# Hybrid mixer block on one core: the linear mixer's loop on 64x64 tiles, the state-space mixer's masked sums made once, and the delta rule's closing part inside the next mixer's projection

## The chip, the cores and the metric

The program runs on one core of one Trainium2 chip. The metric is the device time of one execution in microseconds, lower being better. TensorE is called PE here, its weight loads PEld, VectorE DVE, ScalarE ACT, GpSimd POOL and SyncE SP. All data is float32.

## The reference, cut to what matters

One transformer-like block: four token mixers of 256 channels each read the same normed activations (256 context tokens and 1024 tokens, 10 tiles of 128), and a mixture of experts with 64 experts follows. The change touches the mixers only. Each is a recurrence run forward and backward over chunks of 64 tokens, with 4 heads of 64 channels.

```python
def gla_core(q, k, v, gk, s0):                       # the linear mixer
    b = jnp.cumsum(gk, axis=3)
    q_t, k_t, k_s = q * jnp.exp(b), k * jnp.exp(-b), k * jnp.exp(b_last - b)
    att = jnp.where(incl, jnp.einsum('bnhid,bnhjd->bnhij', q_t, k_t), 0.0)
    o_intra = jnp.einsum('bnhij,bnhjv->bnhiv', att, v)
    def step(s, xs):
        o_n = jnp.einsum('bhid,bhdv->bhiv', q_n, s)
        s = s * dec_n[..., None] + jnp.einsum('bhjd,bhjv->bhdv', k_n, v_n)

def ssd_core(x, a, bm, cm, s0):                      # the state-space mixer
    acum = jnp.cumsum(ac, axis=-1)
    seg = acum[..., :, None] - acum[..., None, :]
    lmat = jnp.exp(jnp.where(incl, seg, -jnp.inf))
    dte = jnp.exp(acum[..., -1:] - acum)
    cd = jnp.exp(acum[..., -1])

def deltanet_mixer(...):                             # the gated delta rule
    o, st = bidir(gdn_core, ...)
    y = head_rms(o, lp['dn_norm_g']) * jax.nn.silu(z)
```

## The kernel before, in words

The mixers run one after the other as phases: `gla` (linear mixer), `mamba` (state-space mixer), `deltanet` (gated delta rule), `rwkv`. A phase ends with a barrier of all engines and the freeing of its semaphores; inside it there are blocks, and every block also starts and ends together on all engines. Each engine runs its own list of instructions, written out by hand in program order, and waits on counting semaphores. All buffers lie in one `arena`; PSUM is eight banks of 128x512, `k.ps[0]` to `k.ps[7]`. A float32 product shows in the trace as two loads and two matmuls, so 16 products of the program are 32 rows there.

A mixer first projects the activations (long rows of 128x512 products) and then runs a loop over 10 steps `i`. In each step two tiles of 128 tokens are handled, one forward (`d = 0`) and one backward (`d = 1`). Steps 0 and 1 are context and only move the state; steps 2 to 9 are `live` and also give outputs.

**Linear mixer loop (L527 to L724).** PE does, per live step: `cumulate(i + 2)` (L499), `scores(i, 0)` (L544), `updates(i)` (L558), `scores(i, 1)`, and for each direction `turn(i + 1, d)` (L536) and `results(i, d)` (L569 and L575). A pair of 64-token chunks is treated as one 128x128 tile: the scores of a head are a 128x128 product of which the mask `k.glamask` keeps the two diagonal blocks; to hold the two heads of a pair apart, the turned queries `QT` are stored with zeros in the other head's rows, by three ACT copies a direction (L635 to L637). DVE masks the scores (L686), moves the state through both chunks (L697 to L713), scales the next queries and keys (`scale`, L656 and L658) and copies the results out (L722). ACT also makes the exponents (L602, L603). PE's `scores` of direction 0 comes before `updates`, and the mask of direction 0 stands before the state work on DVE.

**State-space loop (L1016 to L1146).** Per step and direction, `sums(i, d)` makes three narrow products of the decays with masks (L1022: inclusive, strict and all-ones), then, if live, four 128x128 products (L1026) and two grams (L1031). DVE copies the narrow sums to `SM` (L1102) and caps four differences (`capped`, L1106). ACT takes the exponential `EX` of the sums (L1081), makes `XD` (L1076, inputs times step size) and `XE` (L1085, `XD` times a column of `EX`), and the exponential of the capped differences (L1090). DVE multiplies (`mix`, L1112) and, after PE's `products(i, d)` (L1047, L1050, L1055), closes the step (`close`, L1120 to L1129). PE's order is sums(i+1,0), products(i,0), sums(i+1,1), products(i,1); `sums(i+1,d)` waits for `mix(i,d)`, because both use the banks `k.ps[d]` and `k.ps[2+d]`.

**Delta rule's closing part (`turned_out`, L2038 to L2090).** After the loop's block a block of its own squares, sums and norms the output (DVE, L2079 to L2083), turns it with 64 products (PE, L2071), gates it (DVE, L2089) and writes it to `mixed_turned` (SP, L2059). Then the phase ends and `rwkv` starts: SP loads the low-rank weights `WL` (L2141), and PE needs them for its first products (L2165, L2169). The projection `mains` is L2226, with the narrow `logits` (L2183, L2186) in between.

## Time and profile before

| | us |
|---|---|
| median of three executions | 2696.27 (2692.99 to 2698.2) |
| the profiled execution, its time | 2702.41 |
| its span in the trace | 2700.5 |
| PE busy in the span | 2483.4 |
| DVE busy | 1513.2 |
| ACT busy | 983.5 |
| POOL busy | 830.1 |

The profiled execution has its own time, 1.9 us above its span and 6.1 us above the median. Time stamps in rows count from the start of the span. "Busy" of PE includes matmuls that stream one behind the other, and so says that PE has work, not that it works at its peak. Granted clock 1.00 is 2.4 GHz and 0.50 is 1.2 GHz.

### The profile page before, as it was taken

The page shows a single profiled execution, that of the slowest core. Times are in us where ns is not written, and L with a number is a line of the kernel's source. Part 1 is how long each engine was busy: PE and PEld are TensorE (multiplying, and loading weights), DVE is VectorE, ACT ScalarE, POOL GpSimd, SP SyncE. Part 2 cuts the span into 40 slices and gives each one's busy share as a digit, 9 for nine tenths or more (in the row PEclk, how much of TensorE's full clock was granted, in tenths as well). Part 3 has the DMA queues.
Part 4 walks back from the last instruction along what each step waited for, and adds up shares of the span by engine and source line. Part 5 has one row for each costly group of instructions (what it writes and reads, how often), then busy time and mean ns, then how long its engine had stood idle before and what let it go on. Part 6 is the DMA issues. An engine that isn't in the chain of part 4 may idle for free. (4 is left out here: it accounts for less than half of the span.)

```text
span 2700.5 us, 72223 instructions
## 1 busy us (share of the span) xinstructions
PE 2483.4 (92%) x27163; PEld 1367.8 (51%) x27164; DVE 1513.2 (56%) x2615; ACT 983.5 (36%) x1707; POOL 830.1 (31%) x656
## 2 busy tenths in 40 slices
PE   4999999999799699899879779899999999999976
PEld 2447548745599545799734343233333333333332
DVE  3105464854578603566534566566666666666538
ACT  3513214512222113333211125455555555555422
POOL 1000000000255100111000005566666666666564
PEclk9999998998999899899989889999999999999989
DMA  6001222020000110000123237999989899684177
GB/s 241 28 0 51 92 65 66 33 94 32 2 4 4 38 39 0 3 5 4 55 94 105 113 142 310 340 347 359 359 322 343 332 342 345 254 306 153 71 285 299
DMA packets 109434, 410.20 MB, mean 152 GB/s; under 512 B 20953, under 2 KB 37035, under 8 KB 84140
## 3 DMA queue, kind: packets, MB, share of 16 engines
q1 hardware_dynamic: 76972, 289.81, 29.3%
q0 software_dynamic: 20736, 75.51, 7.2%
q10 hardware_dynamic: 11520, 41.95, 3.9%
q8 instruction: 153, 2.51, 0.4%
q14 instruction: 53, 0.43, 0.0%
HBM read 347.45 MB, written 59.77 MB: 151 GB/s over the span
## 5 line engine op out<-in xcount | busy, mean ns | idle before, releaser
L3323 PE MATMUL bank<-arena 128*32 x1280 | 568.9, 598 | 10.5 <-SPq L68 7.6
L3325 PE MATMUL bank<-arena 128*32 128x512 f32 x3840 | 570.0, 598 | 0.0
L3284 POOL COPY arena<-arena 128x2048 f32 x240 | 448.7, 1903 | 332.1 <-PE bank L3357 326.7
L3323 PEld LDWEIGHTS bank<-arena 128*32 128x32 f32 x1280 | 134.9, 110 | 359.5 <-issue 350.4
L3354 PE MATMUL bank<-arena 128*32 x640 | 289.4, 595 | 5.5 <-POOL arena L3284 5.5
L3357 PE MATMUL bank<-arena 128*32 128x512 f32 x1920 | 290.4, 595 | 0.0
L3478 DVE COPY arena<-arena 128x2048 f32 x80 | 134.8, 1684 | 206.8 <-PE bank L3325 188.4
L3415 ACT COPY arena<-arena 128x2048 f32 x80 | 152.2, 1902 | 169.0 <-PE bank L3325 140.7
L3274 POOL DMA_INDIRECT arena<-normed_rows,arena x80 | 164.2, 2053 | 118.3 <-DVE arena L3462 106.3
L1281 PE MATMUL bank<-arena 64*64 64x64 f32 x4480 | 165.8, 220 | 13.8 <-DVE arena L1353 5.4
L3354 PEld LDWEIGHTS bank<-arena 128*32 128x32 f32 x640 | 70.3, 110 | 197.9 <-issue 197.4
L1281 PEld LDWEIGHTS bank<-arena 64*64 64x64 f32 x4480 | 151.2, 136 | 19.3 <-DVE arena L1353 6.5
L3421 ACT COPY arena<-arena 128x2048 f32 x80 | 152.2, 1903 | 0.0
L3325 PEld LDWEIGHTS bank<-arena 128*32 128x32 f32 x3840 | 150.7, 110 | 0.0
L1522 PE MATMUL bank<-arena 128*128 128x512 f32 (+1 forms) x320 | 132.3, 570 | 0.0
L3456 DVE TENSOR_SCALAR arena<-bank,arena 128x128 f32<-128x128 f32 x320 | 109.0, 402 | 40.1 <-PE bank L3308 40.1
L512 PE MATMUL bank<-arena 128*128 128x512 f32 (+1 forms) x320 | 127.3, 552 | 0.0
L2508 POOL TENSOR_TENSOR arena<-arena 128x512 f32<-128x512 f32 x10 | 12.8, 1283 | 368.9 <-DVE arena L2574 255.0
L3390 ACT ACTIVATE arena<-bank,arena 128x128 f32<-128x128 f32 x320 | 121.7, 468 | 3.4 <-PE bank L3308 3.4
L1400 DVE SCALAR_TENSOR_TENSOR arena<-arena 128x945 f32<-128x945 f32 (+2 forms) x96 | 113.8, 1220 | 1.7
L2793 PE MATMUL bank<-arena 128*128 128x512 f32 x256 | 112.2, 596 | 0.0
L1353 DVE TENSOR_TENSOR arena<-arena,bank 128x512 f32<-128x512 f32 x100 | 68.5, 685 | 68.9 <-PE bank L1281 68.3
(554 smaller groups left out, 4457.3 us busy)
## 6 DMA issues: line engine op xcount, KB each, us to landing
arena<-in_exp_w_gate_dram SPq DMA_DIRECT2D x64, 1024.0 KB, 6.3
arena<-in_exp_w_up_dram SPq DMA_DIRECT2D x64, 1024.0 KB, 9.0
arena<-in_exp_w_down_dram SPq DMA_DIRECT2D x64, 1024.0 KB, 9.8
expert_rows<-arena ACTq DMA_DIRECT2D x80, 512.0 KB
arena<-in_w_mod_dram SPq DMA_DIRECT2D x32, 512.0 KB, 4.5
arena<-in_x_dram SPq DMA_DIRECT2D x16, 512.0 KB, 5.7
arena<-in_w_mod_dram SPq DMA_DIRECT2D x8, 1024.0 KB, 18.4
arena<-in_w_in_dram SPq DMA_DIRECT2D x4, 1536.0 KB, 10.2
```

The source lines that it names most:

```text
L512: last = nc.tensor.matmul(k.ps[p % 4][:, 0:width], k.hT[:, c, t * P:(t + 1) * P], W[g][:, c, ws], start=(c == 0), stop=(c == KC - 1))
L1281: last = self.nc.tensor.matmul(self.banks[bank][r, x * HD:(x + 1) * HD], lhsT[r, x], rhs[r, x], start=True, stop=True)
L1522: last = nc.tensor.matmul(k.ps[p % 4][:, 0:w], W[m // 3 % 2][:, c, (m % 3) * P:(m % 3 + 1) * P], k.hT[:, c, a:a + w], start=(c == 0), stop ...
L3274: nc.gpsimd.indirect_dma_start(out=G[:, b.q], out_offset=None, in_=xn_dram, in_offset=bass.IndirectOffsetOnAxis(ap=ID[:, b.q], axis=0)).th ...
L3284: last = nc.gpsimd.tensor_copy(down_copy(u), down_of(slots[u]))
L3323: nc.tensor.matmul(out(SUB - 1), XTT[:, b.q, c, rows(SUB - 1)], W[:, :, c], start=first, stop=end)
L3325: last = nc.tensor.matmul(out(u), XTT[:, b.q, c, rows(u)], WC[:, u, :, c], start=first, stop=end)
L3354: nc.tensor.matmul(ps[6 + half][rows(SUB - 1), :], HT[:, b.q, f, rows(SUB - 1)], W[:, f, c], start=(f == 0), stop=(f == 1))
L3357: last = nc.tensor.matmul(ps[6 + half][rows(u), :], HT[:, b.q, f, rows(u)], WDC[:, u, f, c], start=(f == 0), stop=(f == 1))
L3415: nc.scalar.copy(copy_of(2, LOW), part_of(slot, LOW)).then_inc(lo_a, 1)
L3421: nc.scalar.copy(copy_of(2, HIGH), part_of(slot, HIGH)).then_inc(hi_a, 1)
L3478: nc.vector.tensor_copy(copy_of(0, LOW), part_of(slots[0], LOW))
```

## The change

Three independent edits, in four phases.

1. **Linear mixer.** Scores, results within the chunk and results from the state are made head by head and chunk by chunk, as 64x64 products. `QT` with its zeros and `KT` become one buffer `QKT`, filled by one ACT copy a direction. PE's order becomes updates, scores, cumulate, both turns, results. `results` is now one group for both directions in two halves: the inner one (into bank 4) waits for the masks, and ACT copies it to the output `O`; the part from the state (into the upper half of banks 2 and 3, `px`) waits for the middle state, and DVE adds it to `O`. The masks move behind the middle state on DVE. Because `px` shares its banks with the scores `pa`, `scores(i)` waits for the addition of the step before (`result_out`).
2. **State-space mixer.** All masked sums of all steps are made at the loop's start by five products (`mask_sums`), then one DVE copy, three ACT exponentials and one DVE product (`XS`, the scale of `XE`). `sums` has no narrow products left and is left out for steps 0 and 1; `XE` is made from `T` and `XS`, `XD` only in live steps, and `XE` not in the last step.
3. **Delta rule and rwkv.** The block `turned_out` is gone. Its work becomes the class `TurnedPost`, called inside rwkv's projection: the norm at the start of DVE's list, the turning behind the first four `mains` products on PE, in bank 7, the gating on DVE and the writing at the end of SP's list. `logits` therefore rotates over three banks instead of four. The low-rank weights `WL` are loaded by SP during the delta rule's loop. ACT waits for the written `mixed_turned` before the copy of the first product of `m == 4`, the thirteenth.

```diff
@@ linear mixer, PE @@
-            def scores(i, d):
-                pe.wait_ge(turned_out, 2 * (i - CT) + d + 1)
-                for h in range(NH):
-                    q = h // 2
-                    last = nc.tensor.matmul(pa[d][:, h * P:(h + 1) * P], KT[:, i % 2, d, q * P:(q + 1) * P],
-                                            QT[:, i % 2, d, h * P:(h + 1) * P], start=True, stop=True)
+            def scores(i):
+                pe.wait_ge(turned_out, 2 * (i - CT) + 2)
+                if i > CT:
+                    pe.wait_ge(result_out, i - CT)
+                for d in range(2):
+                    for q in range(2):
+                        for a in range(2):
+                            r = slice(HD * a, HD * a + HD)
+                            for c in range(2):
+                                j = slice(64 * c, 64 * c + 64)
+                                last = nc.tensor.matmul(pa[a][j, d, q], QKT[r, i % 2, d, (2 + q) * P + 64 * c:(2 + q) * P + 64 * c + 64],
+                                                        QKT[r, i % 2, d, q * P + 64 * c:q * P + 64 * c + 64],
+                                                        start=True, stop=True)
...
+            def results(i):
+                pe.wait_ge(masked, i - CT + 1)
+                if i > CT:
+                    pe.wait_ge(inner_out, i - CT)
...
+                            last = nc.tensor.matmul(po[j, d, h // 2, h % 2],
+                                                    ATT[j, h % 2, d, (h // 2) * HD:(h // 2 + 1) * HD],
+                                                    QKVG[j, t, 2 * GW + h * HD:2 * GW + (h + 1) * HD], start=True, stop=True)
+                last.then_inc(inner, 1)
+                pe.wait_ge(middle, i + 1)
...
+                                last = nc.tensor.matmul(px[a][j, d, q], QKT[r, i % 2, d, q * P + 64 * c:q * P + 64 * c + 64],
+                                                        state_in, start=True, stop=True)
+                last.then_inc(result, 1)
@@ linear mixer, ACT @@
-                        nc.scalar.copy(KT[:, (i + 1) % 2, d].rearrange("p (n m) -> p n m", n=2), turned[:, 2:4])
-                        nc.scalar.copy(to[0:HD, 0::2], turned[0:HD, 0:2])
-                        nc.scalar.copy(to[HD:P, 1::2], turned[HD:P, 0:2]).then_inc(turned_out, 1)
+                        nc.scalar.copy(QKT[:, (i + 1) % 2, d], pt[d]).then_inc(turned_out, 1)
+                if live(i):
+                    act.wait_ge(inner, i - CT + 1)
+                    nc.scalar.copy(both(i), k.ps[4].rearrange("p (d n) -> p d n", d=2)).then_inc(inner_out, 1)
@@ linear mixer, DVE @@
-                    for d in range(2):
-                        last = nc.vector.tensor_copy(O[:, d, tile(i, d) - CT, :], po[d])
+                    dve.wait_ge(inner_out, i - CT + 1)
+                    for a in range(2):
+                        o = both(i).rearrange("p d (q a v) -> p d q a v", q=2, a=2)[:, :, :, a]
+                        last = nc.vector.tensor_tensor(o, o, px[a], ALU.add)
@@ state-space mixer @@
+            def mask_sums():
+                wide = NT * NH
+                for n, mask in enumerate((k.incl, k.strict)):
+                    for d in range(2):
+                        at = (2 * n + d) * wide
+                        nc.tensor.matmul(k.ps[4][:, at:at + wide], mask[d], A[:, :, d * NH:(d + 1) * NH], start=True,
+                                         stop=True)
+                nc.tensor.matmul(k.ps[4][:, 4 * wide:6 * wide], k.ones, A, start=True, stop=True).then_inc(masks_summed, 1)
...
-                for n, mask in enumerate((k.incl[d], k.strict[d], k.ones)):
-                    last = nc.tensor.matmul(k.ps[2 + d][:, GW + n * NH:GW + (n + 1) * NH], mask, A[:, t, r],
-                                            start=True, stop=True)
...
-                    act.wait_ge(sums_out, step(i, d))
-                    nc.scalar.activation(EX[:, i % 2, d], SM[:, i % 2, d], ACT.Exp).then_inc(x_act, 1)
...
-                nc.vector.tensor_copy(SM[:, i % 2, d], k.ps[2 + d][:, GW:GW + 3 * NH]).then_inc(sums_out, 1)
@@ delta rule and rwkv @@
-    turned_out(nc, k, ctx, cr, "dn", O, GZ, norm_g, yT_dram)
...
+        @block.sync
+        def _(sp):
+            for at, w, to in ((B_WL, 64, 0), (B_GL, 64, 64), (B_WL + 64, 32, 128)):
+                sp.dma_start(next_low[:, :, to:to + w], view[:, :, at:at + w]).then_inc(next_in, 16)
+            sp.wait_ge(next_in, 48)
...
+    def turn(self, pe, n, bank):
+        if n == 0:
+            pe.wait_ge(self.ready, 1)
+        else:
+            pe.wait_ge(self.yr, n)
...
+                if p < 4:
+                    post.turn(pe, p, k.ps[7])
...
+                if m == 4:
+                    act.wait_ge(post.written, 64)
...
+            post.rows(dve, chain)
             H.build(nc, k, chain)
...
+            for n in range(4):
+                post.gated(dve, n, k.ps[7])
             dve.wait_ge(out, K_DONE)
```

How the lists change on PE. In the linear mixer's loop before, this is step 2 (L499 cumulate, L544 scores, L558 updates, L536 turn, L569 and L575 results):

```order
L499 MATMUL bank<-arena 128x256 x2
L544 MATMUL bank<-arena 128x128 x4
L558 MATMUL bank<-arena 64x64 x16
L544 MATMUL bank<-arena 128x128 x4
L536 MATMUL bank<-arena 128x128 x4
L569 MATMUL bank<-arena 128x64 x4
L575 MATMUL bank<-arena 64x64 x8
L536 MATMUL bank<-arena 128x128 x4
L569 MATMUL bank<-arena 128x64 x4
L575 MATMUL bank<-arena 64x64 x8
```

And this is the same step of the changed kernel (L568 updates, L553 scores, L503 cumulate, L539 turns, L582 inner results, L594 results from the state):

```order
L568 MATMUL bank<-arena 64x64 x16
L553 MATMUL bank<-arena 64x64 x16
L503 MATMUL bank<-arena 128x256 x2
L539 MATMUL bank<-arena 128x128 x8
L582 MATMUL bank<-arena 64x64 x16
L594 MATMUL bank<-arena 64x64 x16
```

The eight 128x128 scores, eight 128x64 products and sixteen 64-column products have become three groups of sixteen 64x64 products, and the step changes between tile shapes less often.

At the start of rwkv PE's list before is this (L2071 is the delta rule's turning in its own block, L2165 and L2169 the low-rank products, L2226 `mains`, L2183 logits):

```order
L2071 MATMUL bank<-arena 64x64 x64
L2050 UNCONDITIONAL_BRANCH
L2160 UNCONDITIONAL_BRANCH
L2165 MATMUL bank<-arena 128x512 x8
L2169 MATMUL bank<-arena 32x512 x8
L2165 MATMUL bank<-arena 128x512 x8
L2169 MATMUL bank<-arena 32x512 x8
L2165 MATMUL bank<-arena 128x256 x8
L2169 MATMUL bank<-arena 32x256 x8
L2226 MATMUL bank<-arena 128x512 x8
L2183 MATMUL bank<-arena 128x512 x2
```

In the changed kernel it is this (L2201 and L2205 low-rank, L2263 `mains`, L2219 logits, L2114 the delta rule's turning):

```order
L2197 UNCONDITIONAL_BRANCH
L2201 MATMUL bank<-arena 128x512 x8
L2205 MATMUL bank<-arena 32x512 x8
L2201 MATMUL bank<-arena 128x512 x8
L2205 MATMUL bank<-arena 32x512 x8
L2201 MATMUL bank<-arena 128x256 x8
L2205 MATMUL bank<-arena 32x256 x8
L2263 MATMUL bank<-arena 128x512 x8
L2219 MATMUL bank<-arena 128x512 x2
L2114 MATMUL bank<-arena 64x64 x16
L2263 MATMUL bank<-arena 128x512 x8
```

The turning stands in quarters behind the products of the projection instead of ahead of all of them.

## Rows read from the trace of the kernel before

**Rows 1.** The page, busy time and share of the span, by engine.
```profile
PE 2483.4 (92%) x27163; PEld 1367.8 (51%) x27164; DVE 1513.2 (56%) x2615; ACT 983.5 (36%) x1707; POOL 830.1 (31%) x656
```
**Rows 2.** Busy time by stretch: us, PE, PEld, DVE, ACT, POOL, clock, DMA share, GB/s.
```profile
223.70:287.60 63.90, 63.14 (x848) 58.65 (x848) 41.55 (x123) 22.25 (x60) 0.00 (x0) 1.00 0.09 21
443.20:527.30 84.10, 75.77 (x576) 74.07 (x576) 57.45 (x169) 54.41 (x197) 0.20 (x1) 0.88 0.17 54
917.70:938.20 20.50, 6.03 (x128) 5.89 (x128) 12.16 (x19) 0.00 (x0) 0.00 (x0) 0.61 0.15 52
938.20:969.10 30.90, 25.49 (x97) 11.23 (x97) 5.20 (x32) 1.19 (x2) 0.00 (x0) 0.81 0.53 130
969.10:1095.10 126.00, 121.85 (x468) 61.23 (x464) 34.61 (x19) 35.44 (x57) 0.00 (x0) 1.00 0.00 0
```
**Rows 3.** Linear mixer, one live step (248.18 to 256.39), PE's loads grouped by line.
```profile
L544 PEld LDWEIGHTS bank<-arena 128*128 128x128 f32 x16 | 2.0, 191 | 0.1
L569 PEld LDWEIGHTS bank<-arena 128*128 128x128 f32 x16 | 1.9, 192 | 0.0
L575 PEld LDWEIGHTS bank<-arena 128*64 128x64 f32 x32 | 1.7, 137 | 0.1
L536 PEld LDWEIGHTS bank<-arena 128*128 128x128 f32 x8 | 0.9, 140 | 0.1
L499 PEld LDWEIGHTS bank<-arena 128*128 128x128 f32 x4 | 0.7, 189 | 0.1
L558 PEld LDWEIGHTS bank<-arena 64*64 64x64 f32 x32 | 0.6, 133 | 0.1
```
**Rows 4.** Linear mixer, the copies of the results: durations, first and last start.
```profile
L722 DVE COPY arena<-bank x16: 411/420/425, 232.0 to 287.2; 128x256 f32<-128x256 f32 x16
```
**Rows 5.** Linear mixer, ACT's two exponents in the timeline: start, us.
```profile
249.36 0.60 ACT L602 ACTIVATE arena<-bank 128x512 f32<-128x512 f32 x1 [1.78 <-PE bank L499]
249.85 0.59 ACT L603 ACTIVATE arena<-bank 128x512 f32<-128x512 f32 x1
```
**Rows 6.** Delta rule's solve, timeline: 16 products of 64x64, all into one bank.
```profile
905.77 1.01 PEld L1281 LDWEIGHTS bank<-arena 64*64 64x64 f32 x32 [0.82 <-ACT arena L1344]
```
**Rows 7.** State-space loop in the timeline, PE's loads and DVE from 514.3 to 522.4.
```profile
514.31 0.74 PEld L1022 LDWEIGHTS bank<-arena 128*128 128x128 f32 x6 [0.55 <-issue]
514.97 0.97 PEld L1026 LDWEIGHTS bank<-arena 128*128 128x128 f32 x8
...
518.10 0.75 PEld L1022 LDWEIGHTS bank<-arena 128*128 128x128 f32 x6
...
520.49 0.17 DVE L1102 COPY arena<-bank 128x12 f32<-128x12 f32 x1 [0.54 <-PE bank L1031]
...
520.69 1.12 DVE L1106 SCALAR_TENSOR_TENSOR arena<-bank,arena 128x128 f32<-128x128 f32 x4
...
521.74 0.67 DVE L1112 TENSOR_TENSOR arena<-arena,bank 128x512 f32<-128x512 f32 x1
```
**Rows 8.** State-space loop, one period from sums to sums, columns as in rows 2.
```profile
506.09:514.31 8.22, 7.83 (x68) 7.67 (x69) 6.81 (x21) 5.54 (x21) 0.00 (x0) 1.00 0.01 2
```
**Rows 9.** State-space loop's start, the narrow sums of step 3, direction 0.
```profile
461.97 1.35 PEld L1022 LDWEIGHTS bank<-arena 128*128 128x128 f32 x6 [1.59 <-issue]
```
**Rows 10.** Delta rule's closing part and rwkv's start, and deltanet's first products, timeline.
```profile
528.50 6.20 PE L1480 MATMUL bank<-arena 128*32 128x512 f32 x48 [2.24 <-PEq L136]
...
918.28 2.29 DVE L2079 TENSOR_TENSOR arena<-arena 128x2048 f32<-128x2048 f32 x1 [0.60 <-PEq L1732]
...
943.61 10.12 PE L2165 MATMUL bank<-arena 128*128 128x512 f32 x16 [9.61 <-DMA arena<-in_w_in_dram]
...
955.51 7.13 PE L2165 MATMUL bank<-arena 128*128 128x512 f32 x16
...
964.43 3.72 PE L2165 MATMUL bank<-arena 128*128 128x256 f32 x16
...
969.08 7.13 PE L2226 MATMUL bank<-arena 128*128 128x512 f32 x16
```

More of the change, by code:

```diff
@@ L581, in _ @@
             for i in range(NT):
+                updates(i)
+                if live(i):
+                    scores(i)
                 if i + 2 < NT:
                     cumulate(i + 2)
+                if live(i + 1):
+                    for d in range(2):
+                        turn(i + 1, d)
                 if live(i):
-                    scores(i, 0)
-                updates(i)
-                if live(i):
-                    scores(i, 1)
-                for d in range(2):
-                    if live(i + 1):
-                        turn(i + 1, d)
-                    if live(i):
-                        results(i, d)
+                    results(i)
@@ L1057, in products @@
                 last.then_inc(outs, 1)
-            for d in range(2):
-                sums(0, d)
+            mask_sums()
             for i in range(NT):
                 for d in range(2):
-                    if i + 1 < NT:
+                    if live(i + 1):
                         sums(i + 1, d)
+                    if i == 0 and d == 0:
+                        pe.wait_ge(exp_sums, 3)
                     products(i, d)
@@ L2093, in rwkv, with __init__, gains, store @@
-def rwkv(nc, k, ctx, cr, low, w_in, w_w2, w0, a_w2, a0, g_w2, k_k, k_a, r_k, ln_g, ln_b, yT_dram, w_out, WO):
+class TurnedPost:
+    def __init__(self, nc, k, sem, O, GZ, room, cr, norm_g, yT_dram):
+        self.nc, self.k, self.O, self.GZ, self.norm_g, self.yT_dram = nc, k, O, GZ, norm_g, yT_dram
+        self.gain = cr.take(2)
+        self.ss, self.rs, self.rt = (cr.take(2 * XT * 2) for _ in range(3))
+        self.SQ = Carve(cr.arena, room).take(2 * XT, 2, HD)
+        self.YT = Carve(cr.arena, room).take(2, SEQ)
+        self.gain_in, self.ready, self.tr, self.yr, self.written = (
+            sem("dn_gain_loaded"), sem("dn_normed"), sem("dn_turned"), sem("dn_y_ready"), sem("dn_written"))
+    def gains(self, sp):
+        for q in range(2):
+            sp.dma_start(self.gain[:, q:q + 1], self.norm_g[0:1, q * P:(q + 1) * P].rearrange("a p -> p a")).then_inc(
+                self.gain_in, 16)
+    def store(self, sp):
+        for n in range(4):
+            q, c = n // 2, slice((n % 2) * 512, (n % 2 + 1) * 512)
+            sp.wait_ge(self.yr, n + 1)
+            sp.dma_start(self.yT_dram[q * P:(q + 1) * P, c], self.YT[:, q, c]).then_inc(self.written, 16)
+        sp.wait_ge(self.written, 64)
+    def rows(self, dve, chain):
+        nc, O, SQ = self.nc, self.O, self.SQ
+        fl = lambda b: b.rearrange("p c q j -> p (c q) j")
+        chain(nc.vector.tensor_tensor(SQ, O, O, ALU.mult))
+        chain(nc.vector.tensor_reduce(self.ss, fl(SQ), AX.X, ALU.add))
+        chain(nc.vector.tensor_scalar(self.ss, self.ss, 1.0 / HD, RMS_EPS, ALU.mult, ALU.add))
+        rsqrt(nc, chain, self.ss, self.rs, self.rt)
+        nc.vector.tensor_tensor(fl(O), fl(O), over(self.rs, HD), ALU.mult).then_inc(self.ready, 1)
+    def turn(self, pe, n, bank):
[3 more added lines that the diff above has]
+            pe.wait_ge(self.yr, n)
+        q, h = n // 2, n % 2
+        for c in range(8):
+            for a in range(2):
+                r = half(a)
+                last = self.nc.tensor.matmul(bank[r, c * HD:(c + 1) * HD], self.O[r, h * 8 + c, q], self.k.ident[r, r],
+                                             start=True, stop=True)
+        last.then_inc(self.tr, 1)
+    def gated(self, dve, n, bank):
+        if n == 0:
+            dve.wait_ge(self.gain_in, 32)
+        q, c = n // 2, slice((n % 2) * 512, (n % 2 + 1) * 512)
+        dve.wait_ge(self.tr, n + 1)
+        self.nc.vector.scalar_tensor_tensor(self.YT[:, q, c], bank, self.gain[:, q:q + 1], self.GZ[:, q, c], ALU.mult,
+                                            ALU.mult).then_inc(self.yr, 1)
@@ L2095, in rwkv @@
+def rwkv(nc, k, ctx, cr, low, w_in, w_w2, w0, a_w2, a0, g_w2, k_k, k_a, r_k, ln_g, ln_b, yT_dram, w_out, WO, left,
+         dn_norm_g, dn_yT_dram):
     sem = lambda n: ctx.semaphore("rwkv_" + n)
@@ L2307, in _ @@
             chain(TS(col[:, 5], col[:, 1], -1.0, 1.0, ALU.mult, ALU.add))
+            for n in range(4):
+                post.gated(dve, n, k.ps[7])
             dve.wait_ge(out, K_DONE)
```

264 lines of the change are left out of this document (112 added, 152 removed).

## The prediction

> **What bounds the kernel now.** The page comes first: PE is busy for 92% of the span [rows 1], so a stage gains only where PE's own list gets shorter or stops waiting. The second view is the busy time by stretch [rows 2]. In the linear mixer's live steps PE is busy for 63.14 of 63.90 us at clock 1.00: PE's list is the bound, DVE has 41.55 and ACT 22.25. In the state-space loop PE has 75.77 of 84.10 at a mean clock of 0.88: PE and the waits share it. From 917.70 to 938.20, the delta rule's closing block, PE works for 6.03 of 20.50 us. From 938.20 to 969.10, rwkv's low-rank products, it has 25.49 of 30.90 at 0.81, and from there to 1095.10 it has 121.85 of 126.00 at 1.00. The third view is the timeline inside these stretches, for what one step consists of.
>
> **The linear mixer.** A live step takes 7.84 us: (287.2 - 0.3 - 232.0) / 7, since the last start is the second of its pair [rows 4]. Its PE loads are 2.0 scores, 1.9 and 1.7 results, 0.9 turns, 0.7 cumulate, 0.6 updates, 7.8 in all [rows 3]. A group of sixteen 64x64 products (32 rows in the trace) costs 0.6 there with 0.1 behind it when its row halves write different banks, as the updates do. The new scores and the results from the state write that way: 0.7 each. The inner results write both row halves into bank 4; the nearest row is the solve's group, 1.01 [rows 6]. So PE's step becomes 0.7 + 0.7 + 0.8 + 0.95 + 1.0 + 0.7 = 4.85 us (updates, scores, cumulate, turns, inner, state).
>
> That is short enough for another loop to decide. From the start S of a step's scores: 0.7 scores, then 1.15 until ACT starts on the cumulated sums (the step of rows 3 starts at 248.18, the exponent at 249.36 [rows 5]), then five ACT instructions of 128x512 (two exponents, two copies of the turned tiles, the copy of the inner results), 0.49 apart and 0.6 for the last [rows 5], to S + 4.4; then DVE's two additions, as long as the copies they replace, 0.42 each [rows 4] and 0.34 apart; then `result_out` frees the next scores: S + 5.3. DVE in one step has 41.55 / 8 = 5.2 now; two masks of 128x256 take the place of two of 128x512, so about 4.6 after. So 5.3 us a step, an ACT loop with PE just below it. Steps 2 to 7 take 6 x 5.3, step 8 has no exponents (4.4), step 9 nothing to turn (4.3), and the first scores come 1.4 later than now because `updates` goes first: 41.9 against 63.9 [rows 2], 22.0 less. I take off 1.5 for handovers that I left out: **20.5**. The low bound: every 64x64 group at 1.0 and 0.15 more for each of six handovers gives 6.8 us a step less what ACT hides, about 6.3, and a gain of 13. The high bound is 22.5.
>
> Here a rule of the Trainium skill speaks against the change. By the row, 32 loads into one bank take 1.01 us, 32 ns each, where 64-column products behind one another that don't share the array take 1.7 / 32 = 53 ns [rows 3, 6]: the two halves overlap although they share a bank. "TensorEngine Tiling (Array Packing)", Gotcha 1: PSUM Pressure, says that different row tiles cannot access the same PSUM bank at the same time; by that the inner group would take 1.7. The sum goes by the row.
>
> **The state-space loop.** One period is 8.22 us [rows 8]. Its chain: sums of direction 0 and products, 514.31 to 518.10; sums of direction 1, until DVE's copy at 520.49; the copy to 520.69; the caps to 521.74; the mix to 522.41, which frees the next sums. The change takes out of it the narrow products, 514.97 - 514.31 = 0.66, twice, and the copy, 0.20 [rows 7]: 6.7 us. DVE has 6.81 busy in the period [rows 8], 6.4 without the two copies, and must stop once for the products; I take 6.9. ACT goes from 5.54 to 5.1 and stays below. Five periods at full clock (steps 4 to 8) give 5 x 1.32 = 6.6. The period of step 3 runs half at the low clock: 1.35 [rows 9] + 0.66 + 0.2 = 2.2. The last sums and their end give 1.5. Ahead of step 3's sums, three narrow groups of about 1.3 at the low clock go (of `sums(1,1)`, `sums(2,0)`, `sums(2,1)`; those of step 0 are replaced by the five products), and the new start adds a round from PE over DVE, ACT, DVE and ACT, about 1.0 more than now, of which the shorter ACT list of steps 0 and 1 (no `XD`) gives back 0.5: 3.4. Sum 13.7. For the low clock I take off 0.7, since it may last as long as now while less work passes in it: **13**. Bounds: 9, if a period stays at 7.6 because the order on DVE bites, and 14.5, if it reaches 6.7. The additions to ACT and DVE at the start are four small instructions; what hides them is nothing, and they are in the 1.0.
>
> **The delta rule's close.** Its DVE work began at 918.28 in the same phase [rows 10]. Now the phase ends there. At another phase change PE starts 2.24 us after its last product (row at 528.50); here the last scan result on DVE takes some longer, and I put rwkv's first product at 918.9. It was at 943.61, after a wait for the low-rank weights [rows 10]: 24.7 less, both the block and the load. The load, 5.4 us from the phase's start to PE's [rows 2, 10], now lies under the delta rule's loop, whose DMA queues are idle; if that cover failed, the term would lose those 5.4. The first low-rank block took 11.9 (943.61 to 955.51), the second, at full clock, 964.43 - 955.51 = 8.9: 3.0 less if PE starts warm. At 528.50 a phase started with a gap of 2.24 and lost some of that, so I take 2.0. Against it, the turning is four groups of 32 rows at 1.01 [rows 6] in a stretch where PE is the bound (121.85 of 126.00 [rows 2]): 4.0 back. DVE's list: the old block's DVE work is 12.16, and what DVE did from 938.20 to 969.10 is 5.20 [rows 2], so it has made the low-rank copies by 918.9 + 17.4 = 936.3 or just behind the product that they wait for, while PE needs them at 941.5 only; ACT needs `written` twelve products later. All of the norm and the gating is covered by DVE's 34.61 of 126.00 [rows 2]. Behind each `turn` on PE stands the next long product, and a `turn` waits only for a gating of one bank, about as long as the mix of 0.67 [rows 7], behind at least one long product of 7.13 [rows 10]. Three logits banks instead of four: the sigmoid that is waited for is three back, at least one main product earlier. Both at nothing; uncovered they would cost about 0.7 each time, at most 6 in all. Sum 24.7 + 2.0 - 4.0 = **22.7**, between 19 and 24.
>
> **The sum.** 20.5 + 13 + 22.7 = 56.2. The profiled execution goes from 2702.4 to 2646.2; the median stands 6.1 below it, so 2696.3 - 56.2 = **2640**.
>
> **The rivals.**
> - The 64x64 groups of the linear mixer don't overlap: 1.7 each for scores, inner and state [rows 3]. PE's step is 0.7 + 0.8 + 0.95 + 5.1 = 7.6 and the gain there is 2 instead of 20.5: 2659. Against it stands the updates' 0.6 for the same shapes [rows 3]. 5%.
> - The inner group alone is serial (the page's rule above): 1.7 instead of 1.0. It delays ACT's last copy by about 0.4 a step, 3 us: 2643. Against it rows 6. 7%; it lies within the range.
> - The low clock. In the state-space loop it is 0.88 in the mean [rows 2]. The new loops leave PE idle for 6 to 9% of a period (now 1% and 5%). If the linear mixer's loop were granted 0.50, its PE step would be 9.7, 78 us for eight steps against 63.9: 14 lost instead of 20.5 gained, 2675. In the state-space loop, five periods at 6.9 + 5.5 give 2667. "TensorE: Matmul & The Clock Gate", Part 1, says that the clock follows how busy PE has recently been; no row shows a loop of this kind at half. 6% for either.
> - Slower: the low clock holds on through rwkv's projection. In the closing block the clock was 0.61 [rows 2]; each microsecond of full-clock work costs one more. It outweighs the 56.2 only from 112 us of low clock on, nearly the whole 126 us stretch, which now runs at 1.00 after a worse start. All of it would give 2762. 1%.
> - The change does nothing to one of its places: the state-space loop is held by DVE's order, and its periods stay at 8.2; 2647 with what the start and end still give. 5%, within the range.
>
> **How the numbers follow.** The forecast's case has 74%. Its own spread, from the bounds, is 2631 to 2655 (20.5 can be 22.5 or 13, 13 can be 14.5 or 9, 22.7 can be 24 or 19, rarely all at one end). The second and last rivals lie in the same range; outside lie the other three with 12% and some of the spread's tails. So 2631 to 2656 for 8 in 10. A measurement of this kernel tells 0.2%, about 5 us, from no change; the three executions before lie within that. Faster by more than 0.2%: 0.97; within: 0.01; slower: 0.02.
>
> **What would show it.** In the changed trace: the starts of the additions in the linear mixer 5.3 us apart with ACT's copy of the inner results ended last before them (7.8 apart: the first rival; PE's inner group at 1.7 instead of 1.0: the second); scores and state groups at 0.6 each. In the state-space loop, from sums to sums 6.9 us, five products and three exponentials at its start, and step 3's sums about 3.4 earlier counted from the loop's start. No idle PE between the delta rule's last product and rwkv's first beyond 2.5 us, no wait for weights, four groups of 32 rows of about 1.0 behind the first long products. Wrong it would be if the granted clock in either loop reads near 0.5, if PE waits behind a `turn`, or if the low-rank products wait for DVE.

## The result, and the profile after

The changed kernel takes 2637.97 us (median of four runs, 2637.51 to 2639.51), the kernel before 2696.05 us in the same comparison (four runs, 2692.99 to 2698.2): ratio 0.9782, 95% interval 0.9765 to 0.9798, 58.1 us less. Forecast were 2640 and a range of 2631 to 2656. The profiled execution took 2639.51 us with a span of 2637.8, against 2702.41 and 2700.5 before.

Busy time by stretch of the changed kernel, with the columns of [rows 2]: the linear mixer's live steps, the state-space loop, the low-rank products, the projection behind them.
```profile
211.80:264.10 52.30, 41.97 (x1192) 36.15 (x1191) 41.55 (x143) 21.28 (x42) 0.28 (x2) 1.00 0.23 67
...
419.85:485.80 65.95, 57.33 (x466) 55.48 (x466) 54.06 (x151) 44.42 (x156) 0.20 (x1) 0.95 0.22 68
875.30:902.30 27.00, 25.46 (x96) 11.21 (x96) 14.28 (x48) 1.18 (x2) 0.00 (x0) 0.87 0.48 125
902.30:1032.70 130.40, 126.21 (x596) 65.30 (x592) 37.65 (x24) 35.48 (x58) 0.00 (x0) 1.00 0.02 9
```
The stretch from the delta rule's last result to rwkv's main products was 51.4 us long (917.70 to 969.10 [rows 2]) and is 27.0. The state-space loop was 85.3 us from its first load to deltanet's first product (443.2 to 528.50 [rows 2, 10]) and is 65.9. The projection had 126.00 and has 130.34 (902.33 to 1032.67). In the linear mixer PE's list alone no longer bounds the stretch: PE is busy for 41.97 of 52.30 us.

The linear mixer in the changed kernel's timeline, one live step. L582 are the inner results, L594 those from the state, L568 the updates, L553 the scores, L503 the cumulated sums, L539 the turns; L650 copies the inner results on ACT, L676 is the last of DVE's four scalings of the next queries and keys, and L737 are DVE's two additions.
```profile
224.31 1.00 PEld L582 LDWEIGHTS bank<-arena 64*64 64x64 f32 x31 [0.17 <-issue]
...
225.18 0.59 PEld L594 LDWEIGHTS bank<-arena 64*64 64x64 f32 x30
...
225.50 0.59 ACT L650 COPY arena<-bank 128x512 f32<-128x512 f32 x1
...
225.70 0.61 PEld L568 LDWEIGHTS bank<-arena 64*64 64x64 f32 x31
...
225.75 0.42 DVE L676 TENSOR_TENSOR arena<-arena 128x256 f32<-128x256 f32 x1
...
226.22 0.75 DVE L737 TENSOR_TENSOR arena<-arena,bank 128x256 f32<-128x256 f32 x2
...
227.09 0.59 PEld L553 LDWEIGHTS bank<-arena 64*64 64x64 f32 x32 [0.78 <-issue]
...
227.74 0.73 PEld L503 LDWEIGHTS bank<-arena 128*128 128x128 f32 x4
...
228.50 1.01 PEld L539 LDWEIGHTS bank<-arena 128*128 128x128 f32 x8
...
231.59 0.75 DVE L737 TENSOR_TENSOR arena<-arena,bank 128x256 f32<-128x256 f32 x2
```
The additions start right behind ACT's last copy (226.09 against 226.22), and PE's scores wait 0.78 us for them. From one step's additions to the next are 5.37 us; before, from copy to copy, 7.8 [rows 4]. DVE's last scaling ends at 226.17, within 0.1 us of ACT's copy: two branches behind ACT's exponents, the copies on ACT and the scalings on DVE, arrive together. In this step PE and DVE are each busy for 4.7 us and ACT for 2.55.

The state-space loop of the changed kernel: its start (L1039 and L1041 are the five products of the masked sums, L1094 to L1096 the three exponentials, L1077 the first step's products), and two full periods. L1048 are the four 128x128 products of `sums`, which now open a period, and L1147 is DVE's mix.
```profile
419.89 1.28 ACT L1094 ACT_TABLE_LOAD   x1 [0.27 <-PEq L841]
419.89 0.97 PEld L1039 LDWEIGHTS bank<-arena 128*128 128x128 f32 x8 [1.09 <-issue]
...
420.78 0.30 PEld L1041 LDWEIGHTS bank<-arena 128*128 128x128 f32 x2
...
421.27 0.24 DVE L1132 COPY arena<-bank 128x80 f32<-128x80 f32 x1 [0.73 <-PE bank L1041]
421.55 0.24 ACT L1094 ACTIVATE arena<-bank 128x80 f32<-128x80 f32 x1 [0.38 <-DVE arena L1132]
...
422.08 0.24 DVE L1134 TENSOR_TENSOR arena<-arena 128x80 f32<-128x80 f32 x1 [0.56 <-ACT arena L1096]
...
423.49 1.87 PEld L1077 LDWEIGHTS bank<-arena 128*128 128x128 f32 x8 [2.40 <-issue]
...
459.44 0.97 PEld L1048 LDWEIGHTS bank<-arena 128*128 128x128 f32 x8 [0.46 <-DVE arena L1147]
...
466.22 0.97 PEld L1048 LDWEIGHTS bank<-arena 128*128 128x128 f32 x8 [0.46 <-DVE arena L1147]
...
473.00 0.97 PEld L1048 LDWEIGHTS bank<-arena 128*128 128x128 f32 x8 [0.46 <-DVE arena L1147]
```
A period is 6.78 us where it was 8.22 [rows 8]. The narrow sums and DVE's copy are gone from it, and PE waits only for the mix.

rwkv's start in the changed kernel, PE alone, against [rows 10]: the three low-rank blocks and the first main products (L2263).
```profile
876.84 10.13 PE L2201 MATMUL bank<-arena 128*128 128x512 f32 x16 [2.85 <-PEq L136]
...
888.76 7.13 PE L2201 MATMUL bank<-arena 128*128 128x512 f32 x16
...
897.68 3.72 PE L2201 MATMUL bank<-arena 128*128 128x256 f32 x16
...
902.33 7.13 PE L2263 MATMUL bank<-arena 128*128 128x512 f32 x16
```
There is no wait for weights. The gap is 2.85 us instead of 9.61 behind a block of its own, but in this execution the first block is as slow as it was: 11.9 us to the second, the second 8.9.

### The profile page after: what moved, and what is told of

Its sections match the earlier page's. It is cut to its first block and busy times, and to the rows that moved or that the text cites. A ratio compares the mean times of both kernels' runs of the same rounds, so it can differ in the third digit from the quotient of the medians.

```text
span 2637.8 us, 72412 instructions
## 1 busy us (share of the span) xinstructions
PE 2434.2 (92%) x27309; PEld 1316.8 (50%) x27310; DVE 1504.5 (57%) x2601; ACT 967.0 (37%) x1642; POOL 827.8 (31%) x655
## 5 line engine op out<-in xcount | busy, mean ns | idle before, releaser
L3367 PE MATMUL bank<-arena 128*32 x1280 | 570.2, 599 | 11.9 <-SPq L68 8.0
L3500 DVE TENSOR_SCALAR arena<-bank,arena 128x128 f32<-128x128 f32 x320 | 109.3, 404 | 40.7 <-PE bank L3352 40.7
```

The lines of the kernel that those rows point to most:

```text
L3367: nc.tensor.matmul(out(SUB - 1), XTT[:, b.q, c, rows(SUB - 1)], W[:, :, c], start=first, stop=end)
```

## The experiments

**One part of the change at a time.** Three kernels take the hunks of one function each: the linear mixer's, the state-space loop's, and the close of the delta rule. All else is the kernel before.
```diff
# linear_only
+    pa = [k.ps[2 + a][:, 0:GW].rearrange("p (d q n) -> p d q n", d=2, q=2) for a in range(2)]
...
# ssm_only
+            mask_sums()
...
# close_only
+            sp.wait_ge(next_in, 48)
```
The linear mixer alone:

> The kernel before with the linear mixer's edits alone. Theory (PE's list was the bound there, the new step is an ACT loop of 5.3 to 5.4 us): the stretch from the last projection copy to the next phase is 23 us shorter, as in the changed kernel, and the median falls by 20 to 24 us, to about 2673. Rival (the parts help each other, through the clock or the DMA queues): clearly less than 20.

The state-space loop alone:

> The kernel before with the state-space edits alone. Theory (the shorter chain gives 13 as predicted, and a shorter time at the low clock at the loop's start the other 6): the loop is 19 us shorter, the median about 2677, and the low clock ends within 6 us of the loop's start. Rival (the short low-clock time in the changed kernel was the luck of where the loop fell): the low clock lasts 15 to 20 us again, and the loop gains only 13 to 15.

The close alone:

> The kernel before with the delta rule's close inside rwkv's projection and the early load of the low-rank weights alone. Theory: from the last result of the delta rule to rwkv's loop it is 20 us shorter (24.4 ahead of the long products, 4.3 given back by the four groups of turning), the median about 2676. Rival: DVE's norm also delays rwkv's later work, under 17.

| kernel | median us | ratio to before, 95% | gain on that chip |
|---|---|---|---|
| linear_only | 2679.26 | 0.9914 (0.9886 to 0.9942) | 22.2 |
| ssm_only | 2688.38 | 0.9947 (0.9931 to 0.9964) | 13.1 |
| close_only | 2681.73 | 0.992 (0.989 to 0.995) | 19.8 |

The kernel before had a median of 2701.49 us in these comparisons. The three gains add up to 55.1, the whole change gives 58.1. The intervals of the single gains are 4.5 to 8 us wide on either side, so no interaction shows, but one of a few us isn't ruled out.

In the linear mixer's case and the close's the gains are those of the theories (20 to 24, and 20), though the medians stand higher than the 2673 and 2676 that were named, since before was slower in this comparison. The state-space theory missed its median: 13.1 us gained where 19 was expected. In the trace its loop is 65.5 us, 19.8 less than in before's profiled execution, but 14.7 and 16.7 less than the old loop in the traces of linear_only (80.2) and close_only (82.2). The low clock ends at 449.1, 8 us behind the loop's start (theory 6). So the size is near the rival's 13 to 15, while its 15 to 20 us of low clock are not in the trace.

**Quadrants in turn.** The 64x64 products of a group are written one quadrant of the array after the other (scores shown; inner and state results alike):
```diff
-                for d in range(2):
-                    for q in range(2):
-                        for a in range(2):
-                            r = slice(HD * a, HD * a + HD)
-                            for c in range(2):
-                                j = slice(64 * c, 64 * c + 64)
+                for a in range(2):
+                    r = slice(HD * a, HD * a + HD)
+                    for c in range(2):
+                        j = slice(64 * c, 64 * c + 64)
+                        for d in range(2):
+                            for q in range(2):
...
```


> The changed kernel, with the 64x64 products of each group of the linear mixer written one quadrant of the array after the other, where the change writes neighbouring products for different quadrants. The products, their tiles, banks and counts are the same. Theory (the groups are cheap because products that stand next to each other run in different quadrants at the same time): scores, inner results and new states, now 0.60, 0.87 to 1.00 and 0.59 us for 32 loads, go to some 1.6 to 1.9 us each where the quadrant repeats; the step of eight goes from 5.4 us to 8 us or more and the kernel from 2638 us to 2656 to 2664. Rival (the load of a 64x64 tile is cheap by its own size, whatever stands beside it): groups within 0.1 us of what they are, kernel at 2636 to 2640 us.

It took 2654.22 us (2651.73 to 2657.83), ratio 0.9849 (0.9833 to 0.9866). That is 40.7 us less than before on its chip, where the changed kernel is 58.1 less: the order is worth 17 us (16 in the traces' linear mixers). Its timeline, the same step as above (loads, and PE's scores):
```profile
224.84 1.64 PEld L582 LDWEIGHTS bank<-arena 64*64 64x64 f32 x30 [0.17 <-issue]
...
226.51 1.11 PEld L594 LDWEIGHTS bank<-arena 64*64 64x64 f32 x27
...
228.84 1.40 PEld L553 LDWEIGHTS bank<-arena 64*64 64x64 f32 x32 [0.63 <-issue]
...
236.26 1.40 PEld L553 LDWEIGHTS bank<-arena 64*64 64x64 f32 x32 [0.64 <-issue]
```
The same 32 loads take 1.40 us where they took 0.59 (scores), and the step 7.42 us instead of 5.37. So the theory holds: a group is cheap because neighbours run in different quadrants. The cost was less than I expected: the scores stay below 1.6 us, the state group goes only to 1.11, the step of 7.42 is below 8, and the kernel stands 2 us below my range. In the changed kernel the inner group uses two quadrants, those on the diagonal, and takes 0.87 us to the next group's first load (224.31 to 225.18); groups over all four take 0.6; one quadrant at a time takes 1.1 to 1.6. All inner products write bank 4, the two row halves into different partitions of it, and they still overlap.

**The cumulated sums ahead of the scores.** In the changed kernel PE's scores wait 0.78 us for the additions while the cumulated sums, which wait for nothing, stand behind them.
```diff
                 updates(i)
+                if i + 2 < NT:
+                    cumulate(i + 2)
                 if live(i):
                     scores(i)
-                if i + 2 < NT:
-                    cumulate(i + 2)
```


> The changed kernel with PE's cumulate put ahead of scores in the linear mixer. Theory (the step of 5.39 us is the loop scores, cumulate, exponents, copies, inner copy, additions, scores; PE idles 0.7 before the scores): cumulate fills PE's gap and ACT starts earlier, the step falls to about 4.9 to 5.0, 3 us less in all. Rival (PE or DVE already bounds the step at 5.3): no change in the step.

It took 2642.58 us (2637.8 to 2643.12), ratio 0.9774 (0.9745 to 0.9802): no difference from the changed kernel that these runs can tell. In the trace the last additions start at 260.40 instead of 261.96, in a loop whose first ones started 0.45 later, so the loop is 2.0 us shorter: seven steps of 4.8 instead of 5.1 in the mean. The later start is part of the edit, and counted from DVE's last projection copy to the next phase's first product the stretch is 1.7 us shorter. The exponent was on the loop that bounds the step, as the prediction had it. What holds the additions now is DVE's list:
```profile
226.33 0.42 DVE L676 TENSOR_TENSOR arena<-arena 128x256 f32<-128x256 f32 x1
226.67 0.75 DVE L737 TENSOR_TENSOR arena<-arena,bank 128x256 f32<-128x256 f32 x2
```
They follow the last scaling at 0.34 us, as DVE's instructions do behind one another, without a wait.

**The low-rank weights late.** The loads go back to rwkv's start, into the same buffers.
```diff
-            for at, w, to in ((B_WL, 64, 0), (B_GL, 64, 64), (B_WL + 64, 32, 128)):
-                sp.dma_start(next_low[:, :, to:to + w], view[:, :, at:at + w]).then_inc(next_in, 16)
-            sp.wait_ge(next_in, 48)
+            sp.nop(nofuse=True)
...
+            for at, w, to in ((B_WL, 64, 0), (B_GL, 64, 64), (B_WL + 64, 32, 128)):
+                sp.dma_start(WL[:, :, to:to + w], view[:, :, at:at + w]).then_inc(wl_in, 16)
...
+            pe.wait_ge(wl_in, 48)
```


> The changed kernel, with the weights of the five low-rank products loaded when the last mixer starts, as before the change, into the same buffers. The mixer still starts in the place that the change gives it. Theory (the early load of these weights is a part of the gain, since nothing else now covers it): TensorE waits for a DMA ahead of the first block of low-rank products, 3 to 6 us, and the kernel is at 2641 to 2644 us. Rival (the load is covered by the building of the mixed inputs on VectorE, GpSimd and ScalarE ahead of the block): no such wait, 2637 to 2640 us.

It took 2640.89 us (2638.61 to 2649.36), ratio 0.9813 (0.9793 to 0.9834). PE's timeline there:
```profile
881.63 9.13 PE L2202 MATMUL bank<-arena 128*128 128x512 f32 x16 [8.48 <-DMA arena<-in_w_in_dram]
...
906.12 7.13 PE L2264 MATMUL bank<-arena 128*128 128x512 f32 x16
```
The wait for the DMA is back. PE starts 4.8 us later, of which the first block gives back 1.0; the main products start 3.8 us later (906.12 against 902.33). The medians say 2.9 us against the changed kernel's, or 4.1 if each is counted against before on its own chip; the run's spread (2638.61 to 2649.36) covers both. The median lies between the ranges of theory and rival; the wait that the rival denied is in the trace, 5.6 us more than the 2.85 of the changed kernel.

**The kernel before, a second time and with a warm start.** The traces of before and after differ by 19.3 us in the state-space loop, ssm_only's medians by 13.1. Two runs ask whether before's trace is typical, and whether its low clock follows PE's idle time.
```diff
@@ state-space loop of the kernel before, after the first sums
+            for n in range(12):
+                nc.tensor.matmul(k.ps[7][:, GW:GW + P], k.ones, k.ident, start=True, stop=True)
```
The unchanged kernel again:

> The kernel before, unchanged, for a second trace. Theory (the first trace of before is a slow sample of the state-space loop): the loop is some 6 us shorter than 85.3 us, near 79, since the two medians of the state-space part alone and of before differ by 13 us where the two traces differ by 19. Rival (the loop always takes 85 us, and the difference lies elsewhere): 84.5 to 86 us again, with the low granted clock from about 448 to 468 us.

With the products in the gap:

> The kernel before, with 12 products of 128x128 more, into a part of a bank that nothing reads then, right after the first sums of the state-space loop, where TensorE stands idle for 2.6 us ahead of the first step's products. Nothing else differs. Theory (the low granted clock of 447.9 to 468.3 us follows from the idle time ahead of the loop, and takes part in what the loop lost before): with TensorE busy there the low stretch is 5 us or shorter, the loop is 3 to 6 us shorter than 85.3 us, and the kernel is at 2691 to 2695 us on this chip where the kernel before is at 2696 to 2701. Rival (the low stretch comes from the sparse products inside the first steps, or is a chance of one execution): the loop keeps its length within 1 us of what an unchanged execution has, and the median is within 1.5 us of before.

PE's loads of before, run again:
```profile
447.96 0.93 PEld L1055 LDWEIGHTS bank<-arena 128*128 128x128 f32 x4 [2.61 <-ACT arena L1085]
...
459.43 0.97 PEld L1055 LDWEIGHTS bank<-arena 128*128 128x128 f32 x4
462.00 0.74 PEld L1022 LDWEIGHTS bank<-arena 128*128 128x128 f32 x6 [1.59 <-issue]
```
And by stretch, the kernel before with its warm start (columns as in [rows 2]):
```profile
440.70:455.30 14.60, 11.76 (x100) 11.40 (x100) 6.95 (x23) 14.33 (x55) 0.20 (x1) 1.00 0.93 294
455.30:462.40 7.10, 7.01 (x34) 7.04 (x34) 2.68 (x8) 4.64 (x17) 0.00 (x0) 0.52 0.09 18
```
Run again (2697.97 us, one run), the same loads at 462.00 take 0.74 us where they took 1.35 [rows 9]: the clock came back between 6 and 7 us earlier, and the loop was 82.2 us, not 85.3. The theory's direction holds, its 79 does not; the value lies between theory and rival. With the 80.2 and 82.2 named above there are four traces of the old loop; the new one shows 65.5 to 66.0 in ssm_only, cumulate_first and quadrants_in_turn. The mean of the four old ones less 65.9 is 16.6 us.

With the warm start the kernel took 2691.96 us (2690.45 to 2698.74), ratio 0.9986 (0.9968 to 1.0003): not told from before. Its trace is plain all the same. The products fill the gap, the clock stays at 1.00 up to 455.3, and then, behind the next gap (2.63 us at 455.36), it falls for 7.1 us. The low clock moved with the gap. It did not get as short as the theory had it (5 us or less), and the loop of 81.4 us is 3.9 us shorter than in before's first trace but only 0.8 shorter than in its second.

**The changed kernel with its gaps filled.** Ten such products behind the masked sums in one kernel, eleven at the end of PE's list in the delta rule in another, and both with the cumulated sums first in the third.
```diff
@@ after_warm_start, behind the masked sums
+            for n in range(10):
+                nc.tensor.matmul(k.ps[7][:, GW:GW + P], k.ones, k.ident, start=True, stop=True)
@@ close_warm, end of TensorE's list in the delta rule
+            pe.wait_ge(n_rdy, NT)
+            pe.wait_ge(aq_rdy, NT - FIRST)
+            for n in range(11):
+                nc.tensor.matmul(b_gram[:, 0:2 * HD], k.ident, k.ident, start=True, stop=True)
```
In the state-space loop:

> The changed kernel, with 10 products of 128x128 more right after the masked sums at the start of the state-space loop, where TensorE stands idle for 2.4 us. Theory (there too the low granted clock, 5 us from 423.5 us on, follows the idle time): the low stretch is gone or stands later, at the next gap of over 2 us, and the loop of 65.9 us is at most 2.4 us shorter; kernel 2636 to 2638 us. Rival (the low stretch belongs to the first products of the loop whatever stands ahead of them): low stretch of 5 us in its place, loop within 0.5 us of 65.9.

Ahead of the low-rank products:

> The changed kernel, with 11 products of 128x128 more at the end of TensorE's list in the delta rule, into a bank whose readers are done, where TensorE stands idle for 2.85 us ahead of the last mixer's first low-rank block. Nothing else differs. Theory (the first low-rank block runs at the low granted clock because of that idle time, so my 2.0 us for a warm start were missing): the idle time falls to about 1.5 us, the block from 10.13 us to 8 to 9 us, and the kernel is 1 to 2 us faster than the changed one, 2636 to 2637 us where that is at 2638. Rival (the low clock there comes from the sparse 64x64 products of the last periods, not from the gap): the block keeps its 10 us, kernel at 2637.5 to 2640 us.

All three edits:

> The changed kernel with three edits that the traces point to: the linear mixer's cumulative sums ahead of the scores (last additions of the loop were 2 us earlier with it), the 10 products in the gap of the state-space loop, and the 11 products in the gap ahead of the first low-rank block. Theory: the gains add up, 2.0 + up to 2.4 + 1 to 2 us, so 2632 to 2635 us and ratio 0.975 to 0.9775 where the changed kernel's is 0.9782. Rival (each is lost in the state of the clock elsewhere): 2636 to 2640 us, no different from the changed kernel.

| kernel | median us (lowest to highest) | ratio to before, 95% |
|---|---|---|
| close_warm | 2637.11 (2636.6 to 2638.89) | 0.9781 (0.9759 to 0.9804) |
| after_warm_start | 2635.42 (2633.48 to 2642.21) | 0.978 (0.9751 to 0.9809) |
| all_three | 2635.0 (2632.3 to 2639.37) | 0.9775 (0.9752 to 0.9799) |

The kernel before was at 2694.81 us here. PE's timeline of close_warm (L1891 are the products added):
```profile
873.67 2.72 PE L1891 MATMUL bank<-arena 128*128 128x128 f32 x22
877.61 7.10 PE L2205 MATMUL bank<-arena 128*128 128x512 f32 x16 [1.22 <-PEq L136]
...
886.50 7.13 PE L2205 MATMUL bank<-arena 128*128 128x512 f32 x16
```
The first block takes 8.9 us instead of 11.9, at clock 1.00. The products added are all that differs; all_three's trace shows the same 8.9 behind the same 1.22 us. PE starts 1.0 us later, counted from the delta rule's start, because the eleven products end after DVE's last result; 2.0 us stay. Fewer products might keep more of it, which wasn't tried. How much a colder start costs differs between executions. Behind the same gap of 2.86 us the first block took 11.8 us in after_warm_start, but 10.3 in cumulate_first and 10.4 in quadrants_in_turn, whose first rows are:
```profile
873.40 8.55 PE L2201 MATMUL bank<-arena 128*128 128x512 f32 x16 [2.86 <-PEq L136]
892.70 8.58 PE L2201 MATMUL bank<-arena 128*128 128x512 f32 x16 [2.86 <-PEq L136]
```

The state-space loop by stretch: the changed kernel's first steps, then the whole loop of after_warm_start.
```profile
423.40:429.10 5.70, 5.58 (x26) 5.60 (x27) 2.47 (x7) 5.31 (x24) 0.00 (x0) 0.51 1.04 338
```
```profile
422.00:486.10 64.10, 57.22 (x486) 55.16 (x486) 54.14 (x151) 44.20 (x156) 0.20 (x1) 0.99 0.23 70
```
The low stretch of 5.7 us is gone, the loop is 1.8 us shorter. Most of that is given back right behind it. These are deltanet's first 48 products, in the changed kernel and in after_warm_start, and the clock of the 6.85 us from their start:
```profile
485.85 6.20 PE L1512 MATMUL bank<-arena 128*32 128x512 f32 x48 [2.27 <-PEq L136]
485.85:492.70 6.85, 6.85 (x50) 2.66 (x51) 6.64 (x11) 4.69 (x6) 1.32 (x6) 0.75 0.26 67
```
```profile
486.15 7.41 PE L1514 MATMUL bank<-arena 128*32 128x512 f32 x48 [2.27 <-PEq L136]
486.15:493.00 6.85, 6.85 (x44) 2.04 (x48) 6.64 (x11) 4.09 (x5) 1.31 (x6) 0.57 0.30 68
```
The same products behind the same gap take 1.2 us longer, in all_three too (7.44 us). So of the loop's 1.8 us some 0.6 is left, much as the rival of all_three had it. In all_three the gains in the trace are 1.6 us in the linear mixer, 1.9 in the loop less the 1.2, and 1.7 at rwkv's start, and the span is 2633.0. By its median all_three is 3.0 us below the changed kernel (1.7 if each is counted against before in its own comparison), and the ratios' intervals overlap almost wholly. I would take it as the better version by its trace and not claim it by its time.

## Why the prediction was right

- **Linear mixer, forecast 20.5.** The traces show 23.1 (73.75 us from the same DVE instruction to the next phase's first product, then 50.66), the medians 22.2. The step was put at 5.3 us and is 5.37 to 5.4. The loop that the prediction named is there: ACT's last copy, the additions, PE's scores. It named only one of two branches, though: DVE's four scalings arrive at the additions within 0.1 us of ACT's copy. From the first step's output to the last step's the gain is 19.2 us; 3.8 more stand ahead of the first, about 1.5 more than the sum had there. That is why the 1.5 us taken off for handovers look unspent.
- **"TensorEngine Tiling (Array Packing)", Gotcha 1: PSUM Pressure, of the Trainium skill** says that different row tiles can't access one bank at the same time. By that the inner group, whose row halves share a bank, would take 1.7 us, an estimate from [rows 3]. The trace has 0.87 to 1.00, and quadrants_in_turn shows what no overlap costs: 1.64. Here the measurement decides against the rule as it stands; no run here has both row halves write the same partitions of a bank.
- **State-space loop, forecast 13.** The medians of ssm_only say 13.1, interval 9.7 to 18.6 (0.0036 to 0.0069 of 2701.49); the traces 16.6 in the mean and 19.3 for the profiled pair. A full period was put at 6.9 and is 6.78, 7.2 us for five. The start is where I was low: the first load to the sums of step 3 went from 18.76 to 12.41 us, 6.35 less where I had 3.4, and the period of step 3 from 11.25 to 6.78, 4.5 less where I had 2.2; the end gave 1.3 where I had 1.5. So the loop of the traces gained 3.6 to 6.3 us more than forecast, and that the medians of ssm_only meet the 13 is not a confirmation of its terms. The step of the prediction that failed is its sentence "For the low clock I take off 0.7, since it may last as long as now". The low stretch went from 20 us in the profiled execution (14 us in the second) to 5.7 us. ACT's table load also moved: it stood behind ACT's first `XD` (445.27 to 446.55 in the trace of before) and now begins with the phase (419.89); no run separates what that gave from what the shorter low clock gave.
- **The close, forecast 22.7.** The stretch to the main products fell by 24.4 us, less 4.3 given back in the projection (forecast 4.0): 20.1, and close_only's medians say 19.8. The 24.7 for the block and the load held. The term "so I take 2.0" for a warm start was wrong in its size: in the profiled execution it is zero, the first block took 11.9 us as before, and 1.3 to 1.6 in the traces of close_only, cumulate_first and quadrants_in_turn. In all of them the granted clock fell behind the gap of 2.85 us; in close_warm, with 1.22, it didn't. The early load is worth 3.8 us of the 24.4 (low_weights_late), where I had put 5.4 at risk; part of the low clock passes in the wait (0.68 in the mean from 872 to 881.6), and the first block then loses less, 10.9 us instead of 11.9.
- **The rivals.** None came in. The 64x64 groups overlap, the loops run at clock 1.00, but for the state-space loop's first steps, although PE is idle for a fifth of the linear mixer's stretch (the prediction had 6 to 9% of a period; a live step has 0.67 of 5.37 us, 12%), PE waits behind no `turn`, and the order on DVE doesn't hold the periods.
- **The sum.** By the traces 23.1 + 19.3 + 20.1 = 62.5 of the 62.7 us between the two spans. By the medians it is 58.1. The difference is mostly before's profiled execution, which ran 6.4 us above its median, where the changed kernel's ran 1.5 above; 3.1 us of the 6.4 is its long low clock in the state-space loop. That the total is met within 2 us owes something to luck. By the medians of the parts, the linear mixer's forecast is 1.7 us too low, the close's 2.9 too high and the state-space loop's right, and the errors nearly cancel.
- **Slips of the working.** The lower end of the range, 2631, does not follow from the bounds: 22.5 + 14.5 + 24 is 61, which gives 2635. The measured 2638 lies inside either way. The chances of the forecast's case and the rivals add up to 98%.

## What to carry to other kernels

Follow the loop that remains when the bound engine's list gets short: the step came out right to 0.1 us because ACT's five instructions and the handovers were counted, not PE's products alone. Count every branch of it: here DVE's came out as long, and it is what holds the step when PE's order gets better. Write small products so that neighbours fall into different quadrants; the order of a loop nest was worth 2 us a step here. When a change removes work at a phase's start, count what becomes of the clock: a gap of 2.4 to 2.9 us on TensorE cost 1.5 to 3 more behind it, and cheap products into an idle bank took that back in the trace. Look one phase further before you count it: most of what was won in the state-space loop went at the next gap.

## What the runs showed of the hardware

- 32 loads of 64x64 (16 products) take 0.56 to 0.65 us over four quadrants, 0.87 to 1.00 over two, and 1.11 to 1.64 one quadrant after the other.
- The low clock mostly followed gaps of TensorE. Behind 2.40, 2.61, 2.63 and 2.85 us the granted clock fell to 0.50 to 0.54 for 3 to 14 us (20 in one execution); behind 1.22 us, and in after_warm_start behind 1.92 us, it did not. Behind the 2.42 us ahead of the state-space projection it read 0.50 from 265.1 to 268.4 in the changed kernel, and 1.00 all along in all_three. "TensorE: Matmul & The Clock Gate", Part 1, of the Trainium skill says the clock follows how busy PE has recently been; by that rule, the trace agrees where there are gaps. How long it stays low differs from execution to execution of one kernel: 14 and 20 us in the kernel before.
- The clock also fell without a gap. In deltanet's projection of the changed kernel PE's products follow one another, and while it runs 160 rows with a single moving column (L1523) the clock goes to 0.50. In these rows busy time alone doesn't tell the clock:
```profile
573.01 6.46 PE L1523 MATMUL bank<-arena 64*64 64x1 f32 x160
575.80:582.50 6.70, 6.70 (x74) 5.10 (x73) 6.59 (x9) 0.00 (x0) 0.00 (x0) 0.50 0.01 2
```
- The last stage (from the combine's first product to the end) took 114 to 116 us in most traces, and 122 to 123 in the four that were taken on one chip, whatever the kernel. The median of before was 2701.49 there and 2694.8 to 2696.1 elsewhere. The ratios above compare runs of one chip for that reason; where a variant's median is set beside the changed kernel's, it isn't, and a difference of a few us is then no evidence.
